# Spare products on TensorE ahead of the second and the third norm of a hybrid encoder layer

## What is computed

```python
def modulate(x, g, shift, scale):
    return rms_norm(x, g) * (1 + scale[:, None, :]) + shift[:, None, :]

def residual(x, out, g, gate, weight):
    return x + weight * gate[:, None, :] * rms_norm(out, g)

x = residual(x, swiglu(modulate(x, ...), w_ffn1_in, w_ffn1_out), ...)
heads, new_state = mixer(modulate(x, ...))
x = residual(x, heads @ w_out, ...)
x = residual(x, swiglu(modulate(x, ...), w_ffn2_in, w_ffn2_out), ...)
```

## Time and profile before

| | us |
|---|---|
| median of 3 runs | 1413.08 |
| lowest and highest run | 1409.79, 1415.2 |
| the profiled execution, its own time | 1412.4 |
| its span, from the first to the last instruction | 1410.6 |
| TensorE busy in it | 1299.4 (92%) |

### The profile page before, as it was taken

The page is one execution under the profiler, slowest core; times in us unless marked ns, Lnnn a source line. Parts: engine busy times, 40 slices in busy tenths (PEclk is TensorE's granted clock), DMA queues, the critical chain, the costliest instruction groups (busy, mean ns, idle before and its releaser), DMA issues.

```text
span 1410.6 us, 23706 instructions
## 1 busy us (share of the span) xinstructions
PE 1299.4 (92%) x8072; PEld 1137.0 (81%) x8072; DVE 825.4 (59%) x1445; ACT 572.7 (41%) x1131; POOL 319.1 (23%) x276
## 2 busy tenths in 40 slices
PE   4999999999999977999997678959999999999996
PEld 2889999999778867888885356849999999988885
DVE  2666667676435455334337964348777777754545
ACT  4543434343334355322113464355344434434433
POOL 0443434333100000000011513005344444510000
PEclk9999999999999997999989598989999999999998
DMA  9544545454432421311321432112322332222242
GB/s 317 171 150 149 157 142 161 142 156 128 163 127 81 143 79 50 130 60 60 127 69 37 136 111 76 31 74 60 90 75 73 89 89 78 71 67 74 90 134 112
DMA packets 167003, 152.71 MB, mean 108 GB/s; under 512 B 10361, under 2 KB 139777, under 8 KB 166954
## 3 DMA queue, kind: packets, MB, share of 16 engines
q1 hardware_dynamic: 165610, 148.24, 33.5%
q0 software_dynamic: 1344, 3.81, 0.9%
HBM read 142.72 MB, written 9.05 MB: 108 GB/s over the span
## 4 chain that ended last, share of the span: by engine, by line
PE 80%; DVE 10%; issue 4%; ACT 4%; DMA 2%; DVEq 0%; POOL 0%; SPq 0%; ACTq 0%; POOLq 0%
PE ps L1083 77%; DVE resid L1961 1%; DVE h_sums_lo L1742 1%; DVE w_sums_lo L1742 1%; DVE max_den L2250 1%; DMA resid<-in_x_sample 1%; DMA w_raw<-in_w_ffn_in 1%; DVE w_lo L1742 1%; DVE act_t L1853 1%; DVE probs L2259 1%; DVE silu_gate L1846 1%; ACT x_norm L660 1%; PE ps L1125 1%; DVE y L1924 0%; ACT modulated_pairs L711 0%
## 5 line engine op out<-in xcount | busy, mean ns | idle before, releaser
L1083 PE MATMUL ps<-h_sums_hi,w_sums_hi 128*128 128x320 f32 x1216 | 378.8, 316 | 14.7 <-ACT silu_gate L730 4.7
L1083 PE MATMUL ps<-h_sums_hi,w_sums_lo 128*128 128x320 f32 x1216 | 371.4, 310 | 0.0
L1083 PE MATMUL ps<-h_sums_lo,w_sums_hi 128*128 128x320 f32 x1216 | 371.3, 310 | 0.0
L1083 PEld LDWEIGHTS ps<-h_sums_hi,w_sums_hi 128*128 128x128 f32 x1216 | 227.6, 188 | 31.4 <-issue 20.4
L1742 DVE TENSOR_TENSOR w_lo<-w_raw,w_hi 128x512 fp32r<-128x512 f32 (+3 forms) x106 | 100.0, 944 | 229.2 <-ACT w_hi L804 154.6
L1083 PEld LDWEIGHTS ps<-h_sums_lo,w_sums_hi 128*128 128x128 f32 x1216 | 228.0, 189 | 0.0
L1083 PEld LDWEIGHTS ps<-h_sums_hi,w_sums_lo 128*128 128x128 f32 x1216 | 227.8, 188 | 0.0
L1083 PE MATMUL ps<-w_hi,act_hi 128*128 128x512 f32 x440 | 173.4, 394 | 3.6 <-issue 3.6
L1083 PE MATMUL ps<-w_lo,act_hi 128*128 128x512 f32 x440 | 171.4, 390 | 0.0
L1083 PE MATMUL ps<-w_hi,act_lo 128*128 128x512 f32 x440 | 171.4, 390 | 0.0
L1742 DVE TENSOR_TENSOR w_sums_lo<-w_raw,w_sums_hi 128x512 fp32r<-128x512 f32 x136 | 126.2, 933 | 54.4 <-ACT w_sums_hi L748 44.6
(11 more groups left out here) (325 smaller groups left out, 1872.4 us busy)
## 6 DMA issues: line engine op xcount, KB each, us to landing
w_raw<-in_w_ffn_in SPq DMA_DIRECT2D x88, 512.0 KB, 3.8
w_raw<-in_w_ada SPq DMA_DIRECT2D x28, 1024.0 KB, 5.1
w_raw<-in_w_ffn_out SPq DMA_DIRECT2D x88, 256.0 KB, 2.6
w_raw<-in_w_in SPq DMA_DIRECT2D x10, 1024.0 KB, 5.1
w_raw_start<-in_w_ada SPq DMA_DIRECT2D x8, 1024.0 KB, 7.9
w_raw<-in_w_out SPq DMA_DIRECT2D x4, 1024.0 KB, 5.0
k_cache<-in_cache_k SPq DMA_DIRECT2D x8, 512.0 KB, 4.9
v_cache<-in_cache_v SPq DMA_DIRECT2D x8, 512.0 KB, 3.6
```

Source lines behind the costliest of these rows:

```text
L1083: return pe.matmul(out, lhsT, rhs, start=start, stop=stop)
```

## The change

Ahead of the wait for `x_norm`, TensorE gets 13 plain products of the identity with 256 columns of constants, into bank 6, which the transposes of `k = 0` overwrite. They stand between the steps of the row chain: two at once, one behind `y_rstd`, one behind each of the five `x_new`, one behind each of the last four `x_sq`, one behind `x_rstd`. They raise no semaphore, and nothing reads what they write. `norm` runs twice, so there are 26 of them in all.

```diff
             def norm(p, product):
 
+                def spare(count):
+
+                    for _ in range(count):
+                        mm(PS[:, 6, 0:2 * P], ident, CON[:, CI:CI + 2 * P])
+
+                spare(2)
+                pe.wait_ge(y_rstd, p)
+                spare(1)
+                for t in range(NT):
+                    pe.wait_ge(x_new, NT * (p - 1) + t + 1)
+                    spare(1)
+                for t in range(1, NT):
+                    pe.wait_ge(x_sq, NT * p + t + 1)
+                    spare(1)
+                pe.wait_ge(x_rstd, p + 1)
+                spare(1)
                 pe.wait_ge(x_norm, NT * (p + 1))
```

## The result

The changed kernel takes **1420.1 us** (median of 20 runs). One of the 20, of 1663.87 us at a lower clock, is left out of the comparison; the 19 others lie between 1409.57 and 1430.21, with a median of 1419.31. The kernel before took 1414.52 beside it (20 runs, 1406.05 to 1419.8). The ratio is 1.0042, 95% interval 1.0022 to 1.0061: slower by 0.42%. That is within the half per cent that most of the chance was on, but with the other sign than the forecast's 1410.3, and over the upper end of its range (1416.5).

A forecast was written before the change was run, and what follows sets the result against it. TensorE was taken as busy nearly throughout, losing time in waits for the row chain and at half clock behind them. Gains of 1.52 + 0.62 = 2.14 us off the profiled 1412.4 gave 1410.3 us, range 1405.0 to 1416.5.

The forecast's parts named there:

- the half per cent that most of the chance was on: Whole kernel: 0.90 chance of a time within 7.1 us of the median, 0.07 faster, 0.03 slower.
- where the spares lie: TensorE's queue ahead of the transposes: spares delay no other engine, move no DMA, and end 1.52 us before transposes may start.
- The price of a spare: One 256-column product, two records on TensorE: 0.45 us at full clock (0.45 to 0.57), 0.90 at half clock.
- That they cost nothing: Ahead of both norms' transposes: the row chain covers all 13 spares, otherwise 5.9 us a norm would be paid.
- the third rival: Ahead of each norm's transposes: spares at half clock delay them 1.18 us, 2.36 us in all, giving 1414.8; chance 0.18.
- The transposes at full clock: First five transposes of each norm: 0.71 us instead of 1.33, so the first product moves 0.62 us earlier.
- the first rival: Both norms: full clock holds through the gaps ahead of the products, gaining 4.93 us, so 1407.5; chance 0.20.
- the second: Rival, both norms: transposes alone don't hold the clock, so only first transposes gain, 1.24 us, giving 1411.2; chance 0.20.
- The second norm's 1.52 us: Second norm's transposes and products: gain taken with the first column tile at half clock, between 0.62 and 2.89.
- the worse of two cases: Second norm as profiled before the change: clock still 0.50 from 540.00 to 545.80, first column tile's products taking 3.70 us.
- 0.39 us for 0.62: Third norm: 0.62 us gain taken, with the clock falling again before the products; 2.04 if it held.
- 2.14 us: Whole kernel: total gain forecast, 1.52 in the second norm plus 0.62 in the third.

The follow-up runs named there:

- after_third: The changed kernel as it stands, measured again beside the kernel before: 1415.93 us against 1412.49, ratio 1.0008.
- before_again: The kernel before, unchanged, run once more for a second profile: 1412.36 us beside 1412.88, ratio 0.9991.
- spares_156: The changed kernel plus 26 wait-only TensorE instructions per norm, shifting the loop's code by 156 instructions: 1412.85 us, ratio 0.9996 to the kernel before.
- spares_256: The changed kernel plus 76 wait-only TensorE instructions per norm, shifting the loop's code by 256 instructions: 1409.15 us, ratio 0.997 to the kernel before.
- spares_256_again: Repeat of spares_256, the changed kernel plus 76 wait-only instructions per norm: 1409.42 us, ratio 0.9967 to the kernel before.
- waits_256: The kernel before without spares, plus 128 wait-only TensorE instructions per norm (256 in all): 1410.62 us, ratio 0.9974 to the kernel before.

## Why the prediction was wrong

**The step that failed** is the part on where the spares lie: "No DMA is issued or moved." No DMA of the kernel's was; TensorE's own code loads were, by 104 instructions, and the sum had no term for them. The term is 3 to 12 us in the loop (293.8 to 303.0 against 290.5 to 291.2), by how many turns go by before the rhythm falls back: 4, 6, 8 or 17 in the four profiles, 17 being all that are left behind the third load. What ends it isn't settled. The prediction's last sentence, that a span moved by over 5 us would speak against the argument, came true.

A second place of the same kind stands in the mixer. With a shift of 52 there (six profiles), a code load falls among GpSimd's stores of the rotated keys: the first store takes 5.22 to 5.40 us, and TensorE is 0.8 to 1.0 us later behind it. In the eight profiles with a shift of 0, 78 or 128 no code load falls there, the store takes 3.81 to 4.10, and nothing is late. The stores, as the DMA view shows them in `after_third` and then in `before_again` (the us are the median of those issued in the window: 5.30 and 4.23, then 3.86, 2.80 and 2.30):

```profile
q8 instruction: 1, 0.02, 0.9%
...
out_k_prompt<-rope_in POOLq DMA_DIRECT2D x2, 256.0 KB, 4.8
```

```profile
out_k_prompt<-rope_in POOLq DMA_DIRECT2D x3, 256.0 KB, 2.8
```

The buffer comes free late, and TensorE waits in `after_third` where it doesn't in `before_again`:

```profile
PE ps L1387 <- DVE rope_in L2013: 0.6, 1, 0.6
```

**The price of a spare** was right, at the places named: 0.45 was forecast, and where the last six run end to end at full clock (in `spares_156`) their records start 0.21 to 0.22 us apart, so 0.43 a spare. A spare alone takes 0.70 from its start to its end, with its second record 0.32 behind the first.

**That they cost nothing** held mostly. From the last product ahead of a norm to its first transposes it is 12.9 us in all 12 norms without spares. With them it is 12.8 in 11 of 16, and 13.1 to 13.4 in the other five. In three of these the last six ran at half clock for a part. In the two others, the second norm of `spares_256` and `spares_256_again`, the spares start 2.8 us later, behind the 76 waits, and the first seven ran at half clock. This is the third rival in small: 0.2 to 0.5 us, not 1.18.

**The transposes at full clock** brought the first product forward by 0.52 to 0.60 us in the second norm (6.39 or 6.40 us behind the first transposes without spares, 5.80 to 5.87 with) and by 0.53 to 0.59 in the third (6.72 without, 6.13 to 6.19 with), where 0.62 was forecast. That the clock falls again in the gap ahead of the products was right as well, so the first rival didn't come about; the clock of 0.99 from 536.80 to 543.70, through the transposes, speaks against the second.

**The second norm's 1.52 us** were mis-sized. From the last product ahead of it to its last transposes it takes 28.86 us on average without spares (six profiles) and 28.61 with (eight). The execution that I read had 29.87. Two more without spares are like it (29.97, 30.10), but in three the clock came back earlier by itself (27.73). The forecast took the worse of two cases for the only one. The means differ by 0.25 us where single profiles differ by over 2, so this gain isn't told from none. The third norm's mean went from 30.32 to 29.93, 0.39 us for 0.62. Together this is 0.64 us in place of 2.14. The two pairs of kernels at the same shift don't speak against it, within their scatter of some 5 us to either side: 1416.46 without spares to 1415.93 with, 1410.62 to 1409.42.

**What stays open.** `spares_256` and `waits_256` are 3.3 to 4.6 us under the kernel before, more than the spares are worth. At a shift of 256 the loop has its old places, so it may be the 128 in the mixer, but one profile of each doesn't show it: the mixer took 392.2 and 392.4 us from the second norm's last to the third norm's first transposes with spares, 397.7 in `waits_256`, and 394.8 to 397.7 in the kernels with no shift there. Changes of a few code places were not tried further. `spares_256` is the fastest kernel of this study. As `waits_256` comes within 1.2 us of its repeat without any spare, it owes that more to its waits, or the places of the code behind them, than to its spares.

## What to carry to other kernels

An edit that costs no time on its own engine still moves every later instruction, and with them the moments at which code is loaded: where a loop's weight loads have no slack, look in the DMA view for the queue of instruction loads and for a load that lands late around one, and test the edit against the same number of instructions that do nothing. A chain that just fits into a loop turn (here sums, load, sums) makes a single late load last for many turns; cutting that chain, though it gains nothing by itself, takes the danger away. And one profiled execution shows one of several endings of a clock stall: read a second profile of the kernel before, ahead of pricing it.

## What was not expected of the hardware

- With a code load of 16 KB in it, the loop's third weight load (512 KB) lands 4.65 to 4.76 us behind its issue in place of 3.6 to 3.85 (4.24 in one kernel), and with one among stores of 256 KB the first takes 5.22 to 5.40 in place of 3.81 to 4.10. The loop's second weight load isn't later for one (4.16 to 4.90 with, 4.53 to 4.81 without).
- 104 instructions that only wait cost a kernel of 1412.5 us as much as 26 products and their waits: 1416.46 and 1415.93.
- VectorE's 320-column product takes 1.58 us in place of 0.48 when it starts within GpSimd's fourth sum, which stays at 1.55; GpSimd's second sum takes 1.75 in place of 1.30 when it starts within VectorE's `w_sums_lo`.
